# mLSTM scores as two single-pass products from high and low parts, prepared one head ahead

## The reference

```python
MLSTM_HEADS = 8; MLSTM_QK_DIM = 64; MLSTM_V_DIM = 128; S = 512

qk = silu(centred_depthwise_conv(qk_raw, conv_w, conv_b))      # (S, 1024): 8 heads of q, then 8 of k
q = qk[..., :512].reshape(B, S, 8, 64);  k = qk[..., 512:] * 64 ** -0.5

def step(carry, inp):                                          # run forwards and backwards in time
    b = cumsum(fj); D = where(lower, b[t] - b[s] + ij[s], -inf)
    s = einsum('bhtd,bhsd->bhts', qj, kj) * exp(D - m_t)       # the scores, decayed
    num = einsum('bhts,bhsv->bhtv', s, vj) + ...               # weighted values
    den = sum(s) + ...
    h = num / maximum(abs(den), exp(-m_t))
out = sigmoid(o) * rms_norm(h_fwd + h_bwd) * head_gain @ w_out
```

## Time and profile before

| | us |
|---|---|
| median of three runs | 2169.82 (2167.81 to 2169.9) |
| span of the profiled execution, first to last instruction | 2167.1 |
| TensorE busy | 2089.2 (96%) |
| VectorE busy | 1122.9 (52%) |
| GpSimd busy | 861.8 (40%) |
| ScalarE busy | 722.2 (33%) |
| TensorE busy from 1639.7 to 1711.8, in the mLSTM stage | 72.10 of 72.10 |
| VectorE busy in the same stretch | 43.86 |

### The profile page before, as it was taken

How to read it: one execution, slowest core, us unless ns; L and a number is a source line. 1 busy time by engine, 2 the same in 40 slices (tenths; PEclk the granted TensorE clock), 3 DMA queues, 4 the chain that set the end, 5 groups by cost and what they waited for, 6 DMA issues and landing times.

```text
span 2167.1 us, 26691 instructions
## 1 busy us (share of the span) xinstructions
PE 2089.2 (96%) x10174; PEld 1694.4 (78%) x10174; DVE 1122.9 (52%) x1863; ACT 722.2 (33%) x975; POOL 861.8 (40%) x456
## 2 busy tenths in 40 slices
PE   6999899999999999999999999999999999999998
PEld 5877787976788888875478888887897787888887
DVE  4344566533788895458638676704665653111112
ACT  5343534323323222344533222123253333222221
POOL 2322433722344444432243444443444433444442
PEclk9999999999999999999999999999999999999999
DMA  4322202522455552331045555422332122223322
GB/s 138 108 73 84 69 1 78 161 73 74 158 180 191 193 174 84 99 104 39 1 136 174 184 187 194 136 87 69 106 113 100 35 69 80 93 90 101 103 84 81
DMA packets 225133, 233.14 MB, mean 108 GB/s; under 512 B 4211, under 2 KB 220100, under 8 KB 224908
## 3 DMA queue, kind: packets, MB, share of 16 engines
q1 hardware_dynamic: 225036, 231.81, 33.1%
HBM read 229.55 MB, written 2.24 MB: 107 GB/s over the span
## 4 chain that ended last, share of the span: by engine, by line
PE 87%; DVE 7%; ACT 2%; issue 1%; POOL 1%; DMA 1%; SPq 0%; DVEq 0%; ACTq 0%
PE ps L1954 21%; PE ps L1956 21%; PE ps L1955 21%; PE ps L2003 7%; PE ps L2008 4%; PE ps L2551 2%; PE ps L2565 1%; PE ps L2110 1%; PE ps L2288 1%; POOL wL L596 1%; DVE hnL L1248 1%; ACT wH L723 1%; PE ps L2219 1%; DVE T L1261 1%; PE ps L2101 1%
## 5 line engine op out<-in xcount | busy, mean ns | idle before, releaser
L596 POOL TENSOR_TENSOR wL<-raw,wH 128x1024 fp32r<-128x1024 f32 (+2 forms) x322 | 772.4, 2420 | 1151.2 <-ACT wH L723 1145.4
L723 ACT ACTIVATE wH<-raw 128x2048 fp32r<-128x2048 f32 (+2 forms) x161 | 302.6, 1879 | 492.8 <-PE ps L1956 360.4
L1954 PE MATMUL ps<-hnH,wH 128*128 128x512 f32 x1152 | 455.9, 396 | 2.8 <-POOL wL L596 2.8
L1956 PE MATMUL ps<-hnH,wL 128*128 128x512 f32 x1152 | 449.9, 391 | 0.0
L1955 PE MATMUL ps<-hnL,wH 128*128 128x512 f32 x1152 | 449.0, 390 | 0.0
L1580 DVE SCALAR_TENSOR_TENSOR adacc<-adaw,small,adacc 128x256 f32<-128x256 f32 x336 | 273.7, 815 | 12.0
L1954 PE MATMUL ps<-uH,wH 128*128 128x512 f32 x664 | 262.3, 395 | 2.6 <-DVE uL L1246 1.8
L1956 PE MATMUL ps<-uH,wL 128*128 128x512 f32 x664 | 260.0, 392 | 0.0
L1955 PE MATMUL ps<-uL,wH 128*128 128x512 f32 x664 | 259.6, 391 | 0.0
L1954 PEld LDWEIGHTS ps<-hnH,wH 128*128 128x128 f32 x1152 | 217.1, 188 | 47.9 <-issue 4.5
L1956 PEld LDWEIGHTS ps<-hnH,wL 128*128 128x128 f32 x1152 | 216.6, 188 | 46.0
(11 more groups left out here) (385 smaller groups left out, 2994.0 us busy)
## 6 DMA issues: line engine op xcount, KB each, us to landing
raw<-in_ffn_w_dram SPq DMA_DIRECT2D x60, 1024.0 KB, 5.3
adaw<-in_ada_w_dram SPq DMA_DIRECT2D x48, 1024.0 KB, 7.3
raw<-in_w_dram SPq DMA_DIRECT2D x32, 1024.0 KB, 5.3
raw<-in_w_in_dram SPq DMA_DIRECT2D x14, 1024.0 KB, 5.3
raw<-in_od_w_in_dram SPq DMA_DIRECT2D x12, 1024.0 KB, 5.4
raw<-in_w_xkv_dram SPq DMA_DIRECT2D x8, 1024.0 KB, 5.4
raw<-in_ffn_w_dram SPq DMA_DIRECT2D x8, 768.0 KB, 4.2
raw<-in_ev_w_in_dram SPq DMA_DIRECT2D x5, 1024.0 KB, 5.2
```

The source lines that it names most:

```text
L596: nc.gpsimd.tensor_tensor(wL[n % 2][:, k0:k1, 0:c], raw[n % 2][:, k0:k1, 0:c], wH[n % 2][:, k0:k1, 0:c].bitcast(F32), ALU.subtract).then_i ...
L723: nc.scalar.activation(wH[n % 2][:, 0:kc, 0:c], raw[n % 2][:, 0:kc, 0:c], ACT.Copy).then_inc(w_hi, 1)
L1954: nc.tensor.matmul(out_ap, wh, xh, start=first, stop=False)
L1956: return nc.tensor.matmul(out_ap, wl, xh, start=False, stop=last)
```

## The change

The scores' products are changed, and what they read is prepared one head at a time, two heads ahead:

- ScalarE, `scores_high(h)`: three activations of 64 x 512. The keys of the head in float32r into `skeys[h]`, on the 64 partitions that the head has in `cy` (`own`); the queries in float32r into `squeries[h]` on the same partitions, and the same queries once more on the other 64 partitions (`other`).
- VectorE, `scores_low(h)`: two subtractions of 64 x 512. Keys minus high keys into the other half of `skeys[h]`; queries minus high queries in place into `cy` (seen as float32r by the name `cyL`).
- TensorE: for each block of keys one product over 128 rows, `skeys[h]` by `squeries[h]` (high keys by high queries plus low keys by high queries in one), and one over 64 rows, high keys by low queries. Both are float32r and add up in the same bank. The wait for all silus (`c_silu`) becomes a wait for the head's low parts (`l_lo`).
- The tiles lie in memory that is free at that time: the upper halves of `hs` for heads 0 to 3, and chunks of `cy` that are done with for heads 4 to 7. From head 2 on `scores_high(h)` waits until the scores of head h - 2 are made (`l_qk`).
- Heads 0 and 1 are prepared ahead of the loops, head h + 2 in head h: on ScalarE ahead of `head_squares`, on VectorE behind `heads_out(h, 0)`.

```diff
     cy = place("cy", [P, KC, S], F32, UHOFF)[0]
+    cyL = place("cyL", [P, KC, S], F32R, UHOFF)[0]
+    upper = [AR + 4096 * tb + 2048 for tb in range(TB)]
+    done = [UHOFF + 2048 * c for c in (0, 4, 1, 5)]
+    skeys, squeries = [], []
+    for h in range(ML_H):
+        spare = (upper if h < ML_H // 2 else done)[2 * (h % 2):2 * (h % 2) + 2]
+        skeys.append(place(f"skeys{h}", [P, S], F32R, spare[0])[0])
+        squeries.append(place(f"squeries{h}", [P, S], F32R, spare[1])[0])
...
+            def scores_high(h):
+                if h >= ML_H:
+                    return
+                act.wait_ge(c_silu, KC)
+                if h >= 2:
+                    act.wait_ge(l_qk, TB * (h - 1))
+                nc.scalar.activation(skeys[h][own(h), :], cy[own(h), 4 + h // 2, :], ACT.Copy)
+                nc.scalar.activation(squeries[h][own(h), :], cy[own(h), h // 2, :], ACT.Copy)
+                nc.scalar.activation(squeries[h][other(h), :], cy[own(h), h // 2, :], ACT.Copy).then_inc(l_hi, 1)
...
+            scores_high(0)
+            scores_high(1)
             for h in range(ML_H):
...
                 if h in (0, 3, 5):
                     high(n + 11 + h // 2)
+                scores_high(h + 2)
                 if h >= 2:
                     head_squares(h - 2)
...
+            def scores_low(h):
+                if h >= ML_H:
+                    return
+                dve.wait_ge(l_hi, h + 1)
+                nc.vector.tensor_tensor(skeys[h][other(h), :], cy[own(h), 4 + h // 2, :], skeys[h][own(h), :].bitcast(F32), ALU.subtract)
+                nc.vector.tensor_tensor(cyL[own(h), h // 2, :], cy[own(h), h // 2, :], squeries[h][own(h), :].bitcast(F32),
+                                        ALU.subtract).then_inc(l_lo, 1)
...
+            scores_low(0)
+            scores_low(1)
             for h in range(ML_H):
...
                 if not tail:
                     heads_out(h, 0)
+                    scores_low(h + 2)
                     if h >= 2:
                         head_sums(h - 2)
...
-            pe.wait_ge(c_silu, KC)
-
             def scores_half(h, d):
                 if h >= ML_H:
                     return
-                hp = (h % 2) * 64
+                pe.wait_ge(l_lo, h + 1)
                 for j in range(2 * d, 2 * d + 2):
+                    js = slice(j * P, (j + 1) * P)
                     if h:
                         pe.wait_ge(l_a, 8 * (h - 1) + 4 + j + 1)
-                    nc.tensor.matmul(ps[j][:], cy[hp:hp + 64, 4 + h // 2, j * P:(j + 1) * P], cy[hp:hp + 64, h // 2, :],
-                                     start=True, stop=True).then_inc(l_qk, 1)
+                    nc.tensor.matmul(ps[j][:], skeys[h][:, js], squeries[h][:], start=True, stop=False)
+                    nc.tensor.matmul(ps[j][:], skeys[h][own(h), js], cyL[own(h), h // 2, :],
+                                     start=False, stop=True).then_inc(l_qk, 1)
```

More of the change, by code:

```diff
@@ L361, in bass_block_pair, with own, other @@
     cy = place("cy", [P, KC, S], F32, UHOFF)[0]
+    cyL = place("cyL", [P, KC, S], F32R, UHOFF)[0]
[6 more added lines that the diff above has]
+        squeries.append(place(f"squeries{h}", [P, S], F32R, spare[1])[0])
+    def own(h):
+        return slice((h % 2) * 64, (h % 2) * 64 + 64)
+    def other(h):
+        return own(h + 1)
     hsq = T
@@ L439, in bass_block_pair @@
         mrow_out, bc_in = sem("mrow_out"), [sem(f"bc_in{i}") for i in range(BC_RING)]
+        l_hi, l_lo = sem("l_hi"), sem("l_lo")
         l_qk, l_w, l_a, l_wm, l_o, l_h = sem("l_qk"), sem("l_w"), sem("l_a"), sem("l_wm"), sem("l_o"), sem("l_h")
```

## The result

| | before | after |
|---|---|---|
| median, us | 2169.35 (8 runs, 2167.81 to 2172.09) | 2174.77 (8 runs, 2171.76 to 2178.49) |
| ratio of the runs | | 1.0027, interval 1.0017 to 1.0036 |
| profiled execution; its span | -; 2167.1 | 2174.51; 2172.8 |

The account below looks back on a forecast made before the run. TensorE, busy 96% of the span, was taken to bound the kernel, VectorE the stage's tail. Terms +1.4 - 2.9 - 1.65 - 9.0 + 1.2, say -10.9 us, took 2169.8 to 2158.9, so 2159; range 2155.5 to 2165.5.

Parts of the forecast that it names:

- the start: Start of the mLSTM stage: +1.4 for subtractions, -2.9 for three cheaper halves of scores, -1.65 for a shorter low clock.
- the five heads: From out_rows(0, 0) to out_rows(5, 0), set by TensorE: 63.1 us against 72.1, so -9.0.
- head 5: Tail set by VectorE: two subtractions delay out_rows(6, 0), 9.18 becomes 10.4 us, +1.2.
- behind it: Rest of the tail behind out_rows(6, 0): no preparation left, cheaper scores give nothing, no change counted.
- The price of a product: Scores on TensorE: 0.2325 us per single-pass product, 64 rows too; a half falls from 1.91 to 0.93, by 0.98.
- The bound that I carried: Upper bound on a 64-row single-pass product of scores: a float32 record's 0.4775 us.
- Heads 3 and 4: Two of the five heads, with normed_head on VectorE: 12.88 us each, including a TensorE stall of 0.42 for a decay.
- cost nothing: ScalarE's copies in each head (from 0.93 to 2.6 us) lie ahead of the sums and add no time.
- "held" rivals: GpSimd holds VectorE's subtractions in every head: one held, 2167, chance 0.07; both held, 2182, chance 0.03.
- The clock spell that I shortened to 3.3 us: TensorE's half-clock time at the stage's start: 3.2 us instead of 6.6, worth -1.65.
- The case of 2164.0: Rival "less": low clock as long as now, longer masks, both blocks stalled, one subtraction held once; chance 0.20.
- Dear products: Rival: each record still takes 0.4775, TensorE wins nothing, start and tail losses stay: 2172.4; chance 0.03.

Follow-up runs that it names:

- e1: Changed kernel with the second product also over 128 rows (high by low left out, high by high counted twice): 2160.36 us against 2169.04, ratio 0.9957.
- e2: Changed kernel with each half's products regrouped, both of 128 rows first, then both of 64 rows: 2170.04 us, ratio 1.0000.
- e4: Kernel before with two single-pass 64-row products of the same rounded operands per block, no preparation, low parts left out: 2158.04 us, ratio 0.9941.
- e5: Changed kernel with ScalarE's head_squares(h - 2) ahead of scores_high(h + 2): 2171.86 us against 2168.46, ratio 1.0013.
- e3: Kernel before with the preparation of high and low parts alone, scores still plain float32 products: 2177.36 us, ratio 1.0029.
- e8: As e7, with the three subtractions of heads 2 to 7 on GpSimd, one head later, instead of on VectorE: 2156.61 us, ratio 0.9948.
- e6: Changed kernel with VectorE's two subtractions for head 0 ahead of the second half of the last copy of values: 2170.02 us, ratio 1.0009.
- e7: Changed kernel, all computed over 128 rows by a third VectorE subtraction per head, squares first, head 0's low parts early: 2163.91 us, ratio 0.9981.
- e9: As e8, with GpSimd's weight subtractions (wL) from heads 3 and 5 moved behind the low parts in heads 4 and 6: 2158.41 us, ratio 0.9955.

## Why the prediction was wrong

Against the forecast of -10.9 us the stage went up by 5.6, a miss of 16.5: 3.8 in the start, 8.3 in the five heads, 0.9 in head 5, 3.6 behind it.

**The price of a product is the step that failed.** I took 0.2325 for the 64-row product because two float32 lines with 64 and 128 rows took the same. Those are medians of a product's duration, mostly behind its like. The changed kernel alternates, and what I needed was the price of the boundary, which none of my rows showed apart. The chain of before does show it, in the first product of values behind a half, which takes 0.2 more than the next:

```profile
1664.66 1.91 PE ps L2565 x4
1666.57 0.32 PE ps L1954
1666.89 0.12 PE ps L1955
```

A half fell by 0.42 instead of 0.98. e1, e2 with e4, and after stand at 12.05, 12.83 and 13.61 us a head for none, four and eight changes of rows: 0.195 us each, a straight line. Nine halves on the chain, three in the start and six in heads 0 to 2, by 0.56 make 5.0 of the 16.5. The four in heads 3 and 4 can't be added to that, for there VectorE and its holds set the pace. With the holds gone (e5) they took 13.69 and 13.86, which is close both to the pace of the dear products, 13.6, and to what VectorE needs with cheap ones (e1: 13.8 and 13.9, of which 0.5 and 0.6 are holds). The bound that I carried, 0.4775 for a 64-row product, gives 1.42 a half and is short of 1.49, for the 128-row product behind it is dearer as well. By that bound alone the time would be at most 2159 + 13 x 0.49 = 2165.4, inside the range; it was not joined with any other loss.

The Trainium skill, "TensorE: Matmul & The Clock Gate", section "The mechanism", says that a weight load overlaps running matmuls only when its row group differs. By that rule products with equal rows would be the dear ones. This case's traces show otherwise: 128 rows behind 128 (e1) and 64 behind 64 (e4) took 0.23 us from start to start, with a load of 0.18 to 0.19 for each, and 0.42 where 64 and 128 rows, which differ but share partitions, follow each other (after). The measurement decides.

**Heads 3 and 4: the hold came by another door.** The forecast was 12.88 us each, with a stall of 0.42. They took 14.89 and 15.65, 4.8 more together. e5 takes 3.0 of this back by one move on ScalarE: 2.1 are the two holds, and the rest goes with the spell of low clock at the end of head 4. I had asked whether GpSimd would be at work beside the subtractions, and it was not. I had written that the copies on ScalarE "cost nothing": they don't delay the exponentials that VectorE needs, but they delay `head_squares`, hence `gated_head`, which then falls beside VectorE's smallest operations. I held the "held" rivals to subtractions of 512 columns; a 128 x 4 operation is held until GpSimd's ends, just the same. The Trainium skill, "SBUF — State Buffer", section "SBUF: two separate sides", says of a VectorE operation with two SBUF inputs, or in a 2-port mode, and a GpSimd operation that reads SBUF: whichever starts first blocks the other for its whole instruction. The traces of after, e1, e3 and e8 agree, each held operation ending within 0.03 us of GpSimd's.

**The start.** +1.4 for the subtractions was right (1.43). The three halves of scores gave some 1.3 in place of 2.9, by 0.42 each. The clock spell that I shortened to 3.3 us stayed as long as in before (1632 to 1638 and a part of the 2.6 us ahead of it), worth the 1.65 that I had counted. Some 0.5 of the 3.8 is left that I have not taken apart.

**Head 5 and behind.** I forecast +1.2 for head 5, and it was +2.1: 1.4 for the two subtractions, as e5 and e6 have it alone (12.84 against 11.41), and 0.7 for `out_rows(5, 0)` at the low clock. Behind `out_rows(6, 0)` I forecast nothing, and it was +3.6: 2.2 for `out_rows(6, 0)` at the low clock, behind a TensorE that had waited 1.54 us at 1722.17, and 1.6 for `out_rows(7, 1)` at the low clock (4.11 us in place of 2.47), less 0.2 elsewhere. So falls of the clock that I put at nothing make 4.3 of the 16.5, besides some 1 us in head 4.

**What was right:** the position of each term, the heads that TensorE sets up to head 2, VectorE from head 3 on, and 0.69 a subtraction. The case of 2164.0 joined a low clock at the start, longer masks, stalls and one hold, but with products at 0.2325. Dear products stood alone, at 2172.4. That this is near the measured 2174.8 is chance, for its mechanism, a half that stays at 1.91 us, did not come: a half fell to 1.49. The loss came of dearer products, two held operations and falls of the clock together, and their sum had no case of its own.

**What stays open** is the clock. It fell at the start in before, after, e2, e3 and e5, and stayed at 1.00 in e1, e4, e6, e7, e8 and e9. e1 had the same wait ahead of the scores as after (2.36 us); e6 had the same products and a shorter wait (0.85), and before fell behind a wait of 0.85. So neither the wait nor the products decide alone. In head 3 even the same wait of 0.94 us ahead of the same products had a fall behind it in e6 and none in after. Each is one execution, and no run changed the wait by itself in small steps.

## What to carry to other kernels

Price a product by its neighbours: where 64-row and 128-row products alternated, each change cost some 0.2 us, so write the low operand on both halves and keep all 128 rows, if an idle engine can pay for the extra subtraction. When instructions are put ahead of others on an engine off the chain, follow all that stands behind them to the moment where GpSimd and VectorE meet; the size of VectorE's operation doesn't limit the hold. Where TensorE begins to wait a microsecond, look in the windows behind it for the clock before the sum is closed.

## What the runs showed of the hardware

- A change between 64 and 128 rows cost TensorE some 0.2 us each way at a granted clock of 1.00, on top of 0.23 us for a single-pass product of 512 columns and of 0.12 for one of 256 (e1, e2, e4, after).
- VectorE operations on 128 x 4 values in SBUF, 0.16 us alone, took up to 1.22 us beside a GpSimd operation of 1.3 us (after, e1, e3), and 2.17 beside one of 2.4 (e8), and ended within 0.03 us of it.
- 64 x 512 subtractions took 0.69 us on VectorE (after), and 1.3 us on GpSimd (e9).
- In e6 two subtractions worth 1.4 us, moved ahead of one copy, shortened the start by 4.3 us, with the clock granted at 1.00 where it had been at 0.52 (1632 to 1638 in after).
